# Moving the low weights and the activation halves to other addresses, in a one-core hybrid decoder layer

## What is computed

```python
h = concat([meta, x])                                   # 272 x 2048
h = h + 0.5 * swiglu(rms_norm(h, norm_ffn1), gate1, up1, down1)      # D_FF = 5632
h = h + mixer(rms_norm(h, norm_mix), ...)               # HGRN2 and S5 branches, gates, w_out
h = h + 0.5 * swiglu(rms_norm(h, norm_ffn2), gate2, up2, down2)
return rms_norm(h, norm_final)[:, 16:]

def swiglu(x, w_gate, w_up, w_down):
    return (silu(x @ w_gate) * (x @ w_up)) @ w_down
```

## Time and profile before

| what | value |
|---|---|
| median of 3 executions | 2287.3 us |
| all three | 2282.8, 2287.3, 2287.63 us |
| the profiled execution | 2282.81 us |
| its span, first to last instruction | 2281.1 us |
| busy: TensorE / VectorE / ScalarE / GpSimd | 2273.3 / 1551.6 / 1051.4 / 194.7 us |
| granted TensorE clock, mean | 1.0 of full speed |
| DMA, share of 16 engines | 57.9% on the weight queue |

### The profile page before, as it was taken

How to read it: one execution, slowest core, us unless ns; L and a number is a source line. 1 busy time by engine, 2 the same in 40 slices (tenths; PEclk the granted TensorE clock), 3 DMA queues, 4 the chain that set the end, 5 groups by cost and what they waited for, 6 DMA issues and landing times.

```text
span 2281.1 us, 45701 instructions
## 1 busy us (share of the span) xinstructions
PE 2273.3 (100%) x17054; PEld 2132.1 (93%) x17054; DVE 1551.6 (68%) x2143; ACT 1051.4 (46%) x1336; POOL 194.7 (9%) x267
## 2 busy tenths in 40 slices
PE   9999999999999999999999999999999999999998
PEld 9999999999999999998888899998888888888888
DVE  7555544468654589998988786567666655667654
ACT  6444433445543444445555654455444433444444
POOL 0000010289300000002000000000000000000000
PEclk9999999999999999999999999999999999999999
DMA  7555655555555555554555455666565666656564
GB/s 254 176 177 171 181 175 176 175 173 170 183 171 179 175 153 181 174 171 153 162 165 175 156 180 179 195 181 194 184 194 190 188 190 185 186 184 198 186 186 137
DMA packets 117673, 408.62 MB, mean 179 GB/s; under 512 B 17377, under 2 KB 17633, under 8 KB 117601
## 3 DMA queue, kind: packets, MB, share of 16 engines
q1 hardware_dynamic: 116880, 406.55, 57.9%
q10 hardware_dynamic: 720, 1.08, 0.1%
HBM read 405.48 MB, written 2.10 MB: 179 GB/s over the span
## 4 chain that ended last, share of the span: by engine, by line
PE 95%; DVE 3%; issue 1%; ACT 1%; DVEq 0%; ACTq 0%; POOL 0%; POOLq 0%
PE ps L427 31%; PE ps L422 29%; PE ps L426 17%; PE ps L425 16%; DVE w_lo L1133 1%; ACT w_hi L729 0%; DVE qs L1508 0%; PE ps L398 0%; PE ps L648 0%; DVE ks L1507 0%; DVE ks L1509 0%; DVE qs L1510 0%; PE ps L598 0%; DVE gout L1593 0%; PE ps L587 0%
## 5 line engine op out<-in xcount | busy, mean ns | idle before, releaser
L1133 DVE TENSOR_TENSOR w_lo<-raw,w_hi 128x1024 fp32r<-128x1024 f32 x764 | 952.9, 1255 | 570.4 <-ACT w_hi L729 564.6
L427 PE MATMUL ps<-xs,w_lo 128*128 128x256 f32 (+2 forms) x4416 | 1245.6, 282 | 0.0
L729 ACT ACTIVATE w_hi<-raw 128x1024 fp32r<-128x1024 f32 x764 | 802.0, 1058 | 871.1 <-PE ps L427 860.5
L422 PE MATMUL ps<-xs,w_hi 128*128 128x512 f32 (+1 forms) x2432 | 850.5, 394 | 0.1
L427 PEld LDWEIGHTS ps<-xs,w_lo 128*128 128x128 f32 x4416 | 831.8, 188 | 0.0
L425 PE MATMUL ps<-xs,w_hi 128*128 128x272 f32 (+2 forms) x1984 | 570.5, 288 | 0.0
L426 PE MATMUL ps<-xs,w_hi 128*128 128x272 f32 (+2 forms) x1984 | 570.4, 288 | 0.0
L422 PEld LDWEIGHTS ps<-xs,w_hi 128*128 128x128 f32 x2432 | 456.6, 188 | 104.9 <-issue 1.9
L427 PE MATMUL ps<-hs,w_lo 128*128 (+2 forms) x1408 | 400.4, 284 | 0.0
L425 PEld LDWEIGHTS ps<-xs,w_hi 128*128 128x128 f32 x1984 | 372.8, 188 | 0.4
L426 PEld LDWEIGHTS ps<-xs,w_hi 128*128 128x128 f32 x1984 | 373.0, 188 | 0.1
(11 more groups left out here) (289 smaller groups left out, 1598.2 us busy)
## 6 DMA issues: line engine op xcount, KB each, us to landing
raw<-up SPq DMA_DIRECT2D x176, 512.0 KB, 3.7
raw<-down SPq DMA_DIRECT2D x176, 512.0 KB, 3.6
raw<-gate SPq DMA_DIRECT2D x175, 512.0 KB, 4.2
raw<-w_in SPq DMA_DIRECT2D x168, 512.0 KB, 3.6
raw<-w_out SPq DMA_DIRECT2D x32, 512.0 KB, 4.3
raw<-w_proj SPq DMA_DIRECT2D x24, 512.0 KB, 4.3
raw<-glu_a SPq DMA_DIRECT2D x8, 512.0 KB, 4.1
raw<-glu_b SPq DMA_DIRECT2D x8, 512.0 KB, 3.6
```

The lines of the kernel that those rows point to most:

```text
L422: pe.matmul(ps[:, banks + c, 0:2 * n].rearrange("p (s t) -> p s t", s=2), hi, x, start=start and k == 0, stop=False)
L427: last = pe.matmul(out, lo, xh, start=False, stop=stop and k == KT - 1)
L729: act.activation(w_hi[:, slot, :, :], raw[:, slot, :, :], ACT.Copy).then_inc(hi_ready, 1)
L1133: tt(w_lo[:, slot, :, :], raw[:, slot, :, :], w_hi[:, slot, :, :].bitcast(f32), SUB).then_inc(lo_ready, 1)
```

## The change

The change moves data and alters the address patterns that read and write it. Instruction counts, sizes, queues and waits stay as they are.

- `hgn` (12 floats, allocated as 16) moves between `w_hi` and `w_lo`, so `w_lo` and what follows begin 16 floats further on.
- The pads around `xs` go. `x_home` takes its place, 9216 floats. For the first FFN and the mixer it is read as tiles of 576 floats with the low part at 272 (`xs`); for the output projection and the second FFN as tiles of 512 floats, high and low 256 each with nothing between (`xq`).
- The hidden tiles begin 24 floats inside the region. The first FFN's have 576 floats each with the low part at 272 (`hs`); the second FFN's are 512 each (`hq`).
- `inv` and the scan's tables move further up, and nothing else is done to them.

```diff
-PITCH = 288
+STEP, LOW = 576, 272
@@
         w_hi = sb("w_hi", [P, RING, KT, NC], f32r)
+        hgn = sb("hgn", [P, HEADS])
         w_lo = sb("w_lo", [P, RING, KT, NC], f32r)
         h = sb("h", [P, DT, T])
-        sb("in_front_of_xs", [P, 32])
-        xs = sb("xs", [P, DT, 2, PITCH], f32r)
-        x_hi, x_lo = xs[:, :, 0, :], xs[:, :, 1, :]
-        sb("behind_xs", [P, 32])
+        def pairs(home, tiles):
+            both = home.rearrange("p (k x) -> p k x", k=tiles)[:, :, 0:2 * LOW]
+            return both.rearrange("p k (s t) -> p k s t", s=2)
+
+        x_home = sb("x_home", [P, DT * STEP], f32r)
+        xs = pairs(x_home[:, 0:DT * STEP], DT)
+        xq = x_home[:, 0:0 + DT * 2 * SEQ].rearrange("p (k s t) -> p k s t", k=DT, s=2)
@@
-        TAB = 2 * HT * T + 2016
-        hs = at(0, "hs", [P, HT, 2, T], f32r)
-        h_hi, h_lo = hs[:, :, 0, :], hs[:, :, 1, :]
+        HID = HT * STEP
+        HS = 24
+        TAB = HID + HS + 2016
+        hs = pairs(at(HS, "hs", [P, HT * STEP], f32r)[:, :], HT)
+        hq = at(24, "hq", [P, HT, 2, SEQ], f32r)
+        def x_side(index, side):
+            return xq[:, :, side, :] if index == 2 else xs[:, :, side, :]
+        def h_side(f, side):
+            return hq[:, :, side, :] if f else hs[:, :, side, :]
@@ column_block
-                    unit(j, 4 * q + j, banks, T - c0, rows(xs, 4 * j, c0, T - c0), j == 0, j == 3,
+                    unit(j, 4 * q + j, banks, T - c0, rows(parts, 4 * j, skipped, T - c0), j == 0, j == 3,
@@ ffn: column_block(..., parts=(xs, xq)[f]), and for the down passes
-                        one_pass(index, q, blocks // 2, hs, c0, T - c0,
+                        one_pass(index, q, blocks // 2, (hs, hq)[f], 0, T - c0,
@@
-                one_pass(PASS_OUT + p, Q_OUT + 4 * p, 4, xs, META, SEQ, lambda g: pe.wait_ge(m_ready, g * 2 + 2),
+                one_pass(PASS_OUT + p, Q_OUT + 4 * p, 4, xq, 0, SEQ, lambda g: pe.wait_ge(m_ready, g * 2 + 2),
```

More of the change, by code:

```diff
@@ L119, in program @@
         lb = sb("lb", [P, 2, HEADS])
-        hgn = sb("hgn", [P, HEADS])
         dsk = sb("dsk", [P, UT])
@@ L133, in at @@
                 return c.enter_context(nc.sbuf_tensor(name, shape, dt))
-        TAB = 2 * HT * T + 2016
-        hs = at(0, "hs", [P, HT, 2, T], f32r)
-        h_hi, h_lo = hs[:, :, 0, :], hs[:, :, 1, :]
[L138 to L142, removed]
+        HID = HT * STEP
[7 more added lines that the diff above has]
+            return hq[:, :, side, :] if f else hs[:, :, side, :]
+        sv = at(HID + HS, "sv", [P, 14, ST])
+        lbt = at(HID + HS + 1760, "lbt", [P, 3, HEADS])
+        bd = at(HID + HS + 224, "bd", [P, 2, ST, 2 * GP])
+        btmp = at(HID + HS + 1248, "btmp", [P, ST * 32])
+        bprod = at(HID + HS + 1760, "bprod", [P, ST, GP])
         e_re = at(TAB, "e_re", [P, ST, T])
@@ L157, in program @@
         sx = at(U5 + UT * T + T + 512, "sx", [P, SPU, 2, SEQ])
-        inv = at(U5 + UT * T + T + 512 + SPU * 2 * SEQ, "inv", [P, T])
+        inv = at(TAB - T, "inv", [P, T])
         assert U5 + UT * T + 2 * T + 512 + SPU * 2 * SEQ <= TAB
@@ L436, in rows, with column_block @@
                 return lambda k: halves_of(parts[:, first + k, :, c0:c0 + n])
-            def column_block(q, banks, c0, x_need, between=None, fresh=False, wide=False):
+            def column_block(q, banks, c0, x_need, between=None, fresh=False, wide=False, parts=xs):
+                skipped = 0 if parts is xq else c0
                 for j in range(4):
@@ L530, in block @@
                         pe.wait_ge(gated, b + done + 1)
-                        column_block(b * 2 + q, 0, c0, f * 2 * DT, fresh=mean, wide=f == 1)
+                        column_block(b * 2 + q, 0, c0, f * 2 * DT, fresh=mean, wide=f == 1, parts=(xs, xq)[f])
                         if mean:
@@ L534, in block @@
                         pe.wait_ge(hidden, b + done + 1)
-                        column_block(b * 2 + q + 1, 2, c0, f * 2 * DT, wide=f == 1)
+                        column_block(b * 2 + q + 1, 2, c0, f * 2 * DT, wide=f == 1, parts=(xs, xq)[f])
                     peeled = 0 if first else 1
@@ L749, in upper @@
             def upper(index, c0, k):
-                act.activation(x_hi[:, k, c0:T], h[:, k, c0:T], ACT.Copy, scale=gain[:, index, k:k + 1])\
+                act.activation(x_side(index, 0)[:, k, :], h[:, k, c0:T], ACT.Copy, scale=gain[:, index, k:k + 1])\
                     .then_inc(xhi_ready, 1)
@@ L809, in block @@
                         act.wait_ge(hidden, b + done + 2)
-                        act.activation(h_hi[:, ds(b * 2, 2), c0:T], scr[:, 2:4, c0:T], ACT.Copy).then_inc(hhi_ready, 1)
+                        act.activation(h_side(f, 0)[:, ds(b * 2, 2), :], scr[:, 2:4, c0:T], ACT.Copy).then_inc(hhi_ready, 1)
                     peeled = 0 if first else 1
@@ L1081, in take_merged @@
                     act.wait_ge(merged, 4 * p + j + 1)
-                    act.activation(x_hi[:, 8 * p + 2 * j:8 * p + 2 * j + 2, META:T], ybuf[p][:, 2 * j:2 * j + 2, :],
+                    act.activation(xq[:, 8 * p + 2 * j:8 * p + 2 * j + 2, 0, :], ybuf[p][:, 2 * j:2 * j + 2, :],
                                    ACT.Copy).then_inc(mhi_ready, 1)
@@ L1147, in lower @@
                 dve.wait_ge(xhi_ready, index * DT + k + 1)
-                stt(x_lo[:, k, c0:T], h[:, k, c0:T], gain[:, index, k:k + 1], x_hi[:, k, c0:T].bitcast(f32), MUL, SUB)\
+                stt(x_side(index, 1)[:, k, :], h[:, k, c0:T], gain[:, index, k:k + 1],
+                    x_side(index, 0)[:, k, :].bitcast(f32), MUL, SUB)\
                     .then_inc(x_ready, 1)
@@ L1226, in block @@
                         dve.wait_ge(hhi_ready, b + done + 1)
-                        tt(h_lo[:, ds(b * 2, 2), c0:T], sig, h_hi[:, ds(b * 2, 2), c0:T].bitcast(f32), SUB)\
+                        tt(h_side(f, 1)[:, ds(b * 2, 2), :], sig, h_side(f, 0)[:, ds(b * 2, 2), :].bitcast(f32), SUB)\
                             .then_inc(h_ready, 1)
@@ L1692, in take_proj @@
                     dve.wait_ge(mhi_ready, 4 * p + j + 1)
-                    tt(x_lo[:, t:t + 2, META:T], yy, x_hi[:, t:t + 2, META:T].bitcast(f32), SUB).then_inc(m_ready, 1)
+                    tt(xq[:, t:t + 2, 1, :], yy, xq[:, t:t + 2, 0, :].bitcast(f32), SUB).then_inc(m_ready, 1)
                 plain_pass(Q_PROJ + 3 * p, 3, take_proj)
```

## The result

The changed kernel takes 2260.2 us (median of 4, 2259.3 to 2260.9) against 2285.05 us for the kernel before (median of 4 in the same comparison): a ratio of 0.9891, 95% interval 0.9874 to 0.9908. That is 24.9 us faster. I had forecast 10.7 us and a range whose lower end was 2262. Two of the four executions of the kernel before took 2282.6 and 2282.8 us, the other two 2287.3 and 2287.6, so its median lies between two groups, and the stages are compared in the profiled pair, whose spans differ by 21.9 us, 2281.1 and 2259.2.

A forecast was written before the change was run, and what follows sets the result against it. TensorE was taken as the bound, through how fast one matmul follows another. Gains of 3.4 + 7.3 + 0 = 10.7 us took 2287.3 to 2276.6 us; own range 2269 to 2282, 8 in 10 from 2262 to 2291.

The forecast's parts named there:

- Nothing for the writers: Writes of the hidden tiles: costed at nothing, since TensorE waits for none of them.
- Term A: Both FFN down passes: hidden tiles get the x tiles' phase, steps come to those of gate and up; 3.4 us gained.
- Term B: Wide matmuls of output projection and second FFN: one contiguous run replaces two rows; 7.3 us gained.
- My own sign for the term: Second FFN's timeline: line 422 to line 427 at 226 to 227 ns, the 117 back unchanged.
- Term C: All 768 units: low weights move 16 floats against high ones; taken at 0, bounded at 7.6 us either way.
- The forecast of signs for the stages: First FFN's gate and up stays at 124.4 ns, mixer's wide (c, k) at 346.7; `zs` and `o_hi` show `w_lo` cleanest.
- the fourth: Rival: equal distances keep the weight and activation reads apart for good; 25.5 us gained, 2261.8 us; chance 0.11.
- The third, slower: Rival: units with `xs` slow as weight and activation reads 16 floats apart get in each other's way; 2298.7 us; chance 0.13.
- The first rival: Distances don't matter at all, term A's differences come from something that stays; 2287.3 us; chance 0.13.

The follow-up runs named there:

- e6: The changed kernel with the x tiles 48 and the hidden tiles 8 floats further on; 2287.2 us.
- e3: The changed kernel with wide operands of output projection and second FFN again read as two rows, 64 floats between them, in tiles of 576; 2260.0 us.
- e1: The changed kernel with the low weights' shift undone, so they again begin a multiple of 64 floats from the high ones; 2294.6 us.
- e2: The kernel before with only the low weights shifted 16 floats against the high ones, activations left at their places modulo 64 floats; 2292.6 us.
- e5: The changed kernel with the x tiles 16 and the hidden tiles 32 floats further on; 2307.6 us.
- e13: The changed kernel with the x tiles 8 and the hidden tiles 4 floats nearer to the weights; 2289.0 us.
- e8: The changed kernel with the low weights 32 floats from the high ones (modulo 64) in place of 16; 2281.8 us.
- e11: The changed kernel with a pad of 16 floats in front of the first tensor, shifting everything together; 2261.1 us.
- e10: The changed kernel with two more small float32 matmuls ahead of the output projection; 2259.5 us.

## Why the prediction was wrong

The bound and the view to read were right: addresses alone move the steps, and TensorE's steps set the time, but for 1.3 us in the tail. The size was not, 10.7 us against 24.9 (21.9 in the profiled executions). The direction came out right by luck: it was carried by terms A and B, and neither mechanism held.

- **Nothing for the writers**: right. TensorE's waits are as they were.
- **Term A** (3.4 us, down passes come to the steps of gate and up): they did, but gate and up moved as well, and the passes gained 3.5 + 6.7 = 10.2 us. Its reason, multiples of 16 floats, fell with e6.
- **Term B** (7.3 us for the contiguous read): a wrong mechanism. e3 measured it at nothing. The second FFN's gate and up gained 9.1 us, near the term's number, by the place of the rows. The 6.6 ns that I put down to a row jump were not one: the wide step lost only half of them, 3.3 ns, and with 64 floats between the rows it still did. The sign that I read past stood in rows 8: the wide step of the hidden tiles alternated by tile with the same jump in each, so the place moved it and the jump did not. My own sign for the term, 226 to 227 ns from one line to the next, came true by another cause (226.7), and the step back, which was to stay at 117, fell to 113.3.
- **Term C** (0 us): the step that failed. I argued from nearly equal narrow steps that the distance is nearly free, and let the weights' shift, of which no row told anything, default to zero. It is worth 34 us in the changed kernel (e1) and -9.5 us in the kernel before (e2). My bound of 7.6 us either way was the spread among layouts which all had both weights at one phase; a new relation could leave that spread, and did. The bound also counted only narrow units and the mixer's wide ones. The 275 wide units of the output projection and the second FFN were left out of it, and 27.3 us of the 33.5 that e1 costs in the profiled spans lie in the second FFN.
- **The forecast of signs for the stages**: the mixer was to stay, and lost 0.2 us as a sum; its wide (c, k) went from 347 to about 351 ns, which was the sign that term C was the one to size. The stages `zs` and `o_hi`, which I called the cleanest place to see `w_lo`, would have missed it: 46.9 us became 46.7, and 67.9 became 67.8. The output projection was to gain and lost 0.4, by its rhythm. 1.3 us were given back in the tail by the clock.
- **The rivals**: the fourth, a large gain by equal distances, gave 2261.8, 1.6 us from the result. It had 0.11, and its sum took the row jump at full price, so its number came near by luck. Its reason, equal distances, fails too: in the narrow form of the first FFN all reads lie equally far from the weights loaded beside them at x = 16 (370.0 ns), but also at 32 (e5, 380.0), 0 (e6, 375 to 380) and 8 (e13, 373 to 378). The third, slower, named the right danger (weights and activations read side by side at a bad distance), and e1, e2 and e5 are what it looks like.
- **A sum**: with B from 2.2 to 9 us and C within 3, the forecast's own range comes to 2272 to 2285, not 2269 to 2282. The result lies outside either.

The first rival, that distances don't matter, is out: in e1 only the low weights and `hgn`, which the FFNs don't read, lie elsewhere than in the changed kernel, and a wide (c, k) takes 353.1 ns in place of 340.0. The Trainium skill (TensorE: Matmul & The Clock Gate, "Part 2: What happens when you issue a matmul") has two independent read ports, so that loading the next weights takes no read bandwidth from the running matmul. The runs disagree with what I drew from it, that the place of the weights against the activations is free; whether the ports are where the time goes, they don't show.

Left open is the mechanism. The runs show a function of distances and two rhythms; what in the memory or in TensorE makes it, and why one pair of distances is best, none of them shows. Nor does any separate TensorE's reads of the weights from ScalarE's and VectorE's writes of them, which move to the same addresses. That 64 floats is the period rests on e3, where rows and tiles moved by 64 floats and the steps stayed, and on e8 against e1, where the low weights moved by 32 and the steps changed. I only tried places at 4 to 16 floats from each other, and not all pairs.

## What to carry to other kernels

Where matmuls and weight loads run back to back without a wait, list the start addresses of each matmul's operand and of the weights loaded beside it modulo 256 bytes, and treat that list as a parameter to be swept: here it was worth from -1.1% to +1.1% of the kernel's time with no instruction changed. Sweep the tensors together, since undoing or making one move alone was slower than either end, and never take a moved operand at zero because its old place seemed harmless. A pad tensor and a look at the count of matmuls in a fixed window is all that a try costs, as long as the window holds nothing but the stage's own matmuls.

## What the hardware showed that I had not expected

- The step above bare columns depends on distances modulo 64 floats: a wide (c, k) took 340.0 to 353.8 ns, a narrow one of 272 columns 370.0 to 380.0, at the full clock throughout.
- A four-float move (e13) changed it by 3 to 13 ns; a common shift of everything by 16 floats (e11) by nothing; a 64-float gap within an operand by nothing (e3).
- The same addresses have more than one stable rhythm, 340.0 and 350.0 ns, and two extra matmuls ahead of a stage switched it (e10).
- The tail's transposes took 5.23 us in place of 3.56 where the granted clock fell to its lower level, in a tail whose work was the same. Why it fell is open: e3, with the same steps, kept 3.56.
